# One front instead of three stages: two modulation rows first, the bias between the query and key tiles

## The reference, cut to what matters

```python
ada = jax.nn.silu(c) @ ada_w[l] + ada_b[l]
sh1, sc1, g1, sh2, sc2, g2 = jnp.split(ada, 6, axis=-1)      # six rows of 1024
n1 = rmsnorm(h, norm1_w[l]) * (1.0 + sc1) + sh1
proj = n1 @ w_in[l]                  # 1024 query columns, 1024 key columns, and more
# in the attention, for each query q, key k and head:
bias = bias_table[t5_bucket(positions[k] - positions[q])]    # added to the logits
```

## Time and profile before

| | us |
|---|---|
| median of 3 runs (lowest, highest) | 5376.34 (5373.24, 5382.1) |
| the profiled execution | 5366.34 |
| its span, first to last instruction | 5364.7 |
| PE busy, share of the span | 5029.8, 94% |
| DVE busy, share | 2869.8, 53% |
| ACT busy, share | 1572.6, 29% |

### The profile page before, as it was taken

How to read it: one execution, slowest core, us unless ns; L and a number is a source line. 1 busy time by engine, 2 the same in 40 slices (tenths; PEclk the granted TensorE clock), 3 DMA queues, 4 the chain that set the end, 5 groups by cost and what they waited for, 6 DMA issues and landing times. The chain is left out here.

```text
span 5364.7 us, 69919 instructions
## 1 busy us (share of the span) xinstructions
PE 5029.8 (94%) x25070; PEld 4136.0 (77%) x25070; DVE 2869.8 (53%) x6216; ACT 1572.6 (29%) x2427; POOL 254.4 (5%) x340
## 2 busy tenths in 40 slices
PE   5599979998997998999999999999969999999998
PEld 1388867776886777788888888888858888888887
DVE  6511027776566344466666455555545555555556
ACT  2211125565565332222222222222211111111111
POOL 1100000000333110000000000000000000000000
PEclk8798989999998999999999999999989999999999
DMA  7332123332554552222222243333365555555554
GB/s 292 114 118 89 65 84 122 127 126 102 189 184 144 181 165 75 89 85 91 87 91 95 110 161 140 137 153 144 129 175 142 145 147 142 144 148 142 143 147 132
DMA packets 479906, 710.29 MB, mean 132 GB/s; under 512 B 286432, under 2 KB 334960, under 8 KB 474472
## 3 DMA queue, kind: packets, MB, share of 16 engines
q1 hardware_dynamic: 451080, 598.51, 34.9%
q0 software_dynamic: 22880, 96.79, 5.3%
q10 hardware_dynamic: 5760, 12.59, 0.6%
HBM read 487.32 MB, written 220.49 MB: 132 GB/s over the span
## 5 line engine op out<-in xcount | busy, mean ns | idle before, releaser
L2121 PE MATMUL ph_hid_ps<-ph_n_hi,ph_u_hi 128*128 128x512 f32 x2176 | 855.0, 393 | 8.1 <-ACTq L2196 8.0
L2121 PE MATMUL ph_hid_ps<-ph_n_lo,ph_u_hi 128*128 128x512 f32 x2176 | 847.9, 390 | 0.0
L2121 PE MATMUL ph_hid_ps<-ph_n_hi,ph_u_lo 128*128 128x512 f32 x2176 | 847.8, 390 | 0.0
L2506 PE MATMUL px_out_ps<-px_v_hi,px_weight_hi 128*128 128x512 f32 x2048 | 798.0, 390 | 49.6 <-DVEq L2557 49.6
L2506 PE MATMUL px_out_ps<-px_v_lo,px_weight_hi 128*128 128x512 f32 x2048 | 797.7, 390 | 0.0
L2506 PE MATMUL px_out_ps<-px_v_hi,px_weight_lo 128*128 128x512 f32 x2048 | 797.6, 389 | 0.0
L2585 DVE TENSOR_TENSOR held_tiles<-held_tiles,px_out_ps 128x512 f32<-128x512 f32 x512 | 350.4, 685 | 594.2 <-PE px_out_ps L2506 594.2
L2254 DVE TENSOR_TENSOR ph_u_lo<-ph_u_raw,ph_u_hi 128x1024 fp32r<-128x1024 f32 x136 | 166.7, 1226 | 707.4 <-ACT ph_u_hi L2175 707.0
L2180 ACT ACTIVATE ph_hidden<-ph_hid_ps 128x1024 f32<-128x1024 f32 x128 | 131.2, 1025 | 1209.7 <-PE ph_hid_ps L2121 1209.7
L2506 PEld LDWEIGHTS px_out_ps<-px_v_hi,px_weight_hi 128*128 128x128 f32 x2048 | 385.0, 188 | 129.9 <-DVEq L2557 49.8
L2121 PEld LDWEIGHTS ph_hid_ps<-ph_n_hi,ph_u_hi 128*128 128x128 f32 x2176 | 409.4, 188 | 91.9 <-DVE ph_u_lo L2254 8.3
(11 more groups left out here) (319 smaller groups left out, 7926.2 us busy)
## 6 DMA issues: line engine op xcount, KB each, us to landing
ph_u_raw<-in_tiles SPq DMA_DIRECT2D x136, 512.0 KB, 3.6
scratch_hidden<-ph_hidden SPq DMA_DIRECT2D x128, 512.0 KB, 2.6
scratch_gate_tiles<-ph_gates SPq DMA_DIRECT2D x16, 4096.0 KB, 12.8
px_v_raw<-in_v_experts SPq DMA_DIRECT2D x128, 512.0 KB, 3.5
px_raw<-scratch_hidden SPq DMA_DIRECT2D x128, 512.0 KB, 5.3
px_gate<-scratch_gate_tiles SPq DMA_DIRECT2D x128, 512.0 KB, 6.5
proj_w_ch<-in_w_ch SPq DMA_DIRECT2D x49, 512.0 KB, 3.7
mr_w<-in_ada_w POOLq DMA_DIRECT2D x6, 4096.0 KB, 19.6
```

What stands on the lines that cost most here:

```text
L2121: mm = pe.matmul(hid_ps[r][:, c * HALF:(c + 1) * HALF], u[r][a][:, k, :], n2[b][:, k, c * HALF:(c + 1) * HALF], start=(k == 0 and a + b == ...
L2506: mm = pe.matmul(out_ps[b][:], weight[q][j][wp][:, t * P:(t + 1) * P], v[q][j][vp][:, c * HALF:(c + 1) * HALF], start=(j == 0 and wp + vp ...
```

## The change

Stages one to three become one, `front_and_project` (tiles `fr_`), without barriers between them. Its parts, engine by engine:

- Small constants are laid out on the host into one array `front`, loaded by one DMA; the queries' positions come already repeated.
- `ada_w` is loaded in 12 chunks of 2 MB (three quads of two rows, four chunks each). The four of the first quad go to buffers of their own at once. The other eight go through two buffers, each waiting until the chunk two before it has been multiplied.
- The tokens are multiplied by the norm factor only, turned by PE, and copied to `xT` by ACT (even tiles) and DVE (odd tiles). Afterwards the first quad of rows is computed, turned by four transposes into columns (`cols`), and DVE scales and shifts `xT` block by block (128x512); ACT makes the high and DVE the low part of `n1T`. The adding on POOL is gone.
- Two bias groups come ahead of the turning. The other 62 follow the halves of the 16 query and key tiles, two behind each half. One row chunk follows each of the tiles 1 to 8. The bias results are copied in pieces of up to 512 keys from three PSUM banks.

The core of the diff, the new order on each engine (the long declarations and waits on constants are left out):

```diff
+                def half_tile(n, c):
+                    for k in range(KD):
+                        if n == 0:
+                            pe.wait_ge(n1_lo, c * KD + k + 1)
+                        for a, b in PARTS:
+                            mm = pe.matmul(...)
+                    if c:
+                        mm.then_inc(acc_ready[n % 2], 1)
+                # PE
+                for g in range(AHEAD):
+                    bias_group(g)
+                for t in range(TT):
+                    ...transposes of token tile t
+                for i in range(CHUNKS):
+                    row_chunk(i)
+                pe.wait_ge(first_ready, 1)
+                ...four transposes of the first rows
+                for n in range(TILES):
+                    pe.wait_ge(w_lo[n % 2], n // 2 + 1)
+                    for c in range(2):
+                        half_tile(n, c)
+                        for g in groups_behind(n, c):
+                            bias_group(g)
+                    if 1 <= n <= QUADS * CHUNKS - CHUNKS:
+                        row_chunk(n + 3)
+                # ACT
+                def high(n):
+                    ...
+                        act.wait_ge(w_in[n % 2], n // 2 * 16)
+                        act.wait_ge(acc_ready[n % 2], n // 2)
+                    act.activation(w[n % 2][0][:], w_raw[n % 2][:], ACT.Copy).then_inc(w_hi[n % 2], 1)
+                for n in range(TILES):
+                    for g in groups_behind(n, 0):
+                        take_group(g)
+                    act.wait_ge(acc_ready[n % 2], n // 2 + 1)
+                    act.activation(out[n % 2][:], acc[n % 2][:], ACT.Copy, ...)
+                    if n + 2 < TILES:
+                        high(n + 2)
+                    for g in groups_behind(n, 1):
+                        take_group(g)
+                # DVE
+                def make_steps(g):
+                    if g >= NSTEP:
+                        dve.wait_ge(piece_mm, pieces_until(g - NSTEP + 1))
+                    ...four tensor_scalar of 128 x extent(g), then_inc(steps_ready)
+                def low(n):
+                    dve.wait_ge(w_hi[n % 2], n // 2 + 1)
+                    dve.tensor_tensor(w[n % 2][1][:], ...).then_inc(w_lo[n % 2], 1)
+                full(0)
+                for i in range(2 * KD):
+                    if i + 1 < 2 * KD:
+                        full(i + 1)
+                    dve.wait_ge(n1_hi, i + 1)
+                    dve.tensor_tensor(n1T[1][:, k, cut], xT[:, k, cut], ...).then_inc(n1_lo, 1)
+                for n in range(TILES):
+                    for g in groups_behind(n, 0):
+                        make_steps(g)
+                    if n + 2 < TILES:
+                        low(n + 2)
+                    for g in groups_behind(n, 1):
+                        make_steps(g)
+                # POOL
+                for i in range(6):
+                    load_chunk(i)
+                for n in range(2, TILES):
+                    pool.wait_ge(w_lo[n % 2], n // 2)
+                    pool.dma_start(w_raw[n % 2][:], d["w_ch"][n]).then_inc(w_in[n % 2], 16)
+                    if 6 <= n + 3 < QUADS * CHUNKS:
+                        load_chunk(n + 3)
+        def groups_behind(n, half):
+            at = AHEAD + 4 * n + 2 * half      # AHEAD = 2, NSTEP = 4 buffers of steps
+            return range(at, min(at + 2, GROUPS))
```

More of the change, by code:

```diff
@@ L102, in bucket_starts, with stage_project, front_and_project @@
             for b in range(NB)]
+FRONT_WIDTHS = (P, 1, AH, AH, 1, 3 * KD, KD)
+FRONT_CONSTS = sum(FRONT_WIDTHS)
+FRONT_AT = tuple((sum(FRONT_WIDTHS[:n]), sum(FRONT_WIDTHS[:n + 1])) for n in range(len(FRONT_WIDTHS)))
 def stage_modulation_and_bias(nc, d):
+    pass
+def stage_project(nc, d):
+    with ExitStack() as stack:
+        sp = Space(nc, stack, "proj")
+        with ExitStack() as early:
+            mod_w = early.enter_context(nc.sbuf_tensor("proj_mod_w", [P, 2, 2, 2 * D], F32))
+            xT = early.enter_context(nc.sbuf_tensor("proj_xT", [P, KD, S], F32))
+        n1T = [sp.sb(f"n1T_{part}", [P, KD, S], F32R) for part in ("hi", "lo")]
+        w_ch = [sp.sb(f"w_ch{s}", [P, KD, P]) for s in range(2)]
+        with ExitStack() as tokens:
+            w_tok = [tokens.enter_context(nc.sbuf_tensor(f"proj_w_tok{s}", [P, KD, HALF], F32)) for s in range(2)]
+            w_dt = tokens.enter_context(nc.sbuf_tensor("proj_w_dt", [P, KD, SH], F32))
+            front_and_project(nc, d, n1T, mod_w, xT, w_ch, w_tok, w_dt)
+            project_token_major(nc, d, n1T, w_tok, w_dt, w_ch)
+        attend_and_convolve(nc, d, n1T, w_ch)
+        scan_and_gate(nc, d, n1T, w_ch)
+def front_and_project(nc, d, n1T, mod_w, xT, w_raw, w_tok, w_dt):
     QG = 4
@@ L111, in stage_modulation_and_bias @@
     NJ = QB // QG
-    NBUF = 4
-    N = P // QB // NBUF
-    ROWS = 6
+    NSTEP = 4
+    GROUPS = S // QB
+    AHEAD = 2
     QUADS = 3
-    KC = KD // 2
+    CHUNKS = 4
     TERMS = 3
+    TILES = 2 * AH
+    NBANK = 3
     with ExitStack() as stack:
-        sp = Space(nc, stack, "mr")
-        cT = sp.sb("cT", [P, KD])
+        sp = Space(nc, stack, "fr")
+        consts = sp.sb("consts", [P, FRONT_CONSTS])
+        ident, eps, table, before, first, mod_cols, cT = (consts[:, a:b] for a, b in FRONT_AT)
+        x = sp.sb("x", [P, TT, D])
@@ L138, in stage_modulation_and_bias @@
+        pos_q = sp.sb("pos_q", [P, S // QG], I32)
         pos_k = sp.sb("pos_k", [P, S])
         limit = sp.sb("limit", [P, S // QG])
-        first = sp.sb("first", [P, 1])
-        table = sp.sb("table", [P, AH])
-        before = sp.sb("before", [P, AH])
         diffs_raw = sp.sb("diffs_raw", [P, NB])
         diffs = [sp.sb(f"diffs{n}", [P, NB], BF16) for n in range(TERMS)]
-        steps = [sp.sb(f"steps{s}", [P, NJ, S], BF16) for s in range(NBUF)]
+        w = [[sp.sb(f"w{s}_{part}", [P, KD, P], F32R) for part in ("hi", "lo")] for s in range(2)]
@@ new lines, in front_and_project @@
+        steps = [sp.sb(f"steps{s}", [P, NJ, S], BF16)[:] for s in range(2)] + [
+            x[:, 2 * s:2 * s + 2, :].bitcast(BF16).rearrange("p a (c n) -> p (a c) n", n=S) for s in range(2)]
+        squares = bias_out[1]
+        first_rows = bias_out[1][:, 0:HALF]
+        pos_k_int = out[1][:].bitcast(I32)
+        chunk_to = [w_tok[c][:].rearrange("p k n -> p (k n)").rearrange("p (a n) -> p a n", a=2) for c in range(2)] + [
+            mod_w[:, c, :, :] for c in range(2)]
+        acc = [sp.ps(f"acc{s}", [P, S]) for s in range(2)]
@@ L157, in lane, with pieces, pieces_until @@
+        def pieces(g):
+            return [(c, min(c + HALF, extent(g))) for c in range(0, extent(g), HALF)]
+        def pieces_until(g):
+            return sum(len(pieces(i)) for i in range(g))
+        def groups_behind(n, half):
+            at = AHEAD + 4 * n + 2 * half
+            return range(at, min(at + 2, GROUPS))
         def lane(j):
             return slice(j * NB, j * NB + 1)
[L160 to L166, removed]
@@ L178, in _ @@
[L178 to L188, removed]
@@ new lines, in _ @@
+                for n in range(TILES):
+                    for half in range(2):
+                        if half:
+                            sync.wait_ge(acc_out[n % 2], n // 2 + 1)
+                            sync.dma_start(d["qkT"][n], out[n % 2][:]).then_inc(stored[n % 2], 16)
+                        for g in groups_behind(n, half):
+                            store_group(g)
+                sync.wait_ge(row_step, 6)
+                for j in range(NJ):
+                    sync.dma_start(d["rows"].rearrange("v n -> (v n)").rearrange("(q j n) -> j q n", j=NJ, n=HALF)[j:j + 1, 1:QUADS],
@@ L231, in _ @@
                         st.wait()
[L232 to L243, removed]
@@ L245, in take_rows @@
-                def take_rows(q):
[L246 to L256, removed]
```

520 lines of the change are left out of this document (238 added, 282 removed).

## The result

| | us |
|---|---|
| forecast | 5394, range 5367 to 5420 |
| the new kernel, median of 16 runs | 5383.61 (5379.86 to 5386.16) |
| the kernel before, median of 16 runs | 5376.91 (5367.74 to 5384.3) |
| ratio | 1.0014, interval 1.0007 to 1.0020 |
| span of the profile, after and before | 5380.3 and 5364.7 |

The new kernel is a little slower: 6.7 us by the medians, and 15.6 us by the two profiles; the forecast was 17.4. The interval of the ratio is clear of 1, but 6.7 us is under the 11 us that I had called discernible, so by my own classes the outcome is "same", to which I had given 0.24, and not "slower" with 0.62.

The account below looks back on a forecast made before the run. PE bounds 94% of the span, but not its front. Up to the mark 101+308+20+6.2 = 435.3 against 417.9, +17.4 us: profiled 5366.3 becomes 5384, and 10.0 for the median gives 5394, range 5367 to 5420.

Parts of the forecast that it names:

- the mark: The first token-major matmul, behind which both kernels have the same code: forecast about 435 us against 417.9 before.
- Part 1: Front up to the first tile matmul: loads, early bias pieces, turning, row chunks and a chain, 70 us in all.
- F: Time of the first tile matmul: forecast 70 us, bounds 61 and 78, against 235.0 before.
- Part 2: Tile 0: PE waits for DVE's blocks and the steps behind them; end at F+31 = 101 us, bounds F+27 and F+33.
- Part 3: Tiles to 15: PE waits in each for steps queued behind ACT copy, high part and low part; together 308 us.
- Part 4: PE's clock falls in the waits of nearly each tile: 1.4 us a tile, 20 in all, bounds 0 and 45.
- Part 5: The rest: 6.2 us from tile 15's end to the mark, stores nothing; then the whole sum and the forecast 5394.
- Rival A: Front and tiles: the two gains cancel, about -3 us with the clock alone staying up, 5374; chance 0.20.
- B: Tiles: the bias hides because steps are ready when PE comes to them, 5287; chance 0.10.
- C: Tiles: weights come late behind POOL's row chunk issue, six tiles at 5 us each, +30, 5424; chance 0.12.

Follow-up runs that it names:

- e5: The new kernel with DVE making the steps of tile 0's first two bias groups before it scales the tokens: 5376.52 us.
- e1: The new kernel with the second half's bias steps made before the low part of the weights in DVE's order: 5286.49 us, ratio 0.9841 to the kernel before.
- e3: The new kernel with ACT making the high part of the weights before it copies out the finished tile: 5370.42 us.
- e2: The new kernel with extra PE matmuls, their product overwritten, before the second half's bias groups of tiles 0 to 13: 5366.4 us.
- e9: The new kernel with e1's and e5's orders and POOL issuing each tile's weights ahead of the row chunk: 5281.22 us, ratio 0.9833 to the kernel before.
- e7: The kernel before, unchanged, profiled a third time: span 5376.1 us, DVE beginning at 38.4.
- e11: The kernel before with POOL's third 4 MB row chunk held until the small constants have landed: 5365.55 us, ratio 0.9991 to the kernel before.
- e6: The new kernel with the three order changes of e1, e3 and e5 together: 5284.75 us.

## Why the prediction was right, point by point

The direction is right, the size two and a half times the one measured: 17.4 us against 6.7. On the profiles' own scale, where the sum was made, it is 15.6, and the mark moved by 16.9.

- **Part 1.** F was forecast at 70 and came at 64.2, inside 61 to 78. The tokens landed as forecast (ACT's last square at 36.75), and the fourth bias piece waited 20.32 us on PE for ACT, as told. The square root, 2 us in the sum, took 0.30. But the turning and the row chunks took 12.9 and 7.1 us, not 15.8 and 10: the clock rose during the turning, and from there DVE, which multiplies by the norm factor, set the pace of the turning (PE waits 0.89 to 1.11 for it between tiles). The rows show it by durations (two tiles in 1.97 us, one in 1.94 in the earlier trace rows; a chunk pair in 3.61, the warm value of the earlier trace rows):

```profile
38.77 1.47 PE L323 MATMUL fr_bias_ps<-fr_steps,fr_diffs 128*32 128x512 bf16 x12 [20.32 <-ACT fr_bias_out L392]
...
45.82 1.97 PE L359 MATMUL fr_acc<-fr_consts,fr_x 128*128 128x128 f32 x16 [0.89 <-DVE fr_x L480]
...
52.99 3.61 PE L336 MATMUL fr_row_ps<-proj_w_tok,fr_silu_c 128*1 128x512 f32 x32
```

- **Part 2.** Tile 0 ended 28.1 us behind F, forecast 31 within 27 to 33. DVE made the late steps from 79.6, and the stop was theirs (e5).
- **Part 3.** The step that decides was right. The 14 long waits of PE were 70.5 us; the chains and first groups' steps of the sum are 49.0+24.5 = 73.5. e1 took the wait away and e3 shortened one link by its own length.
- **Part 4.** 20 us were forecast for the clock; e2 bought back 16 to 17. I had read the earlier trace rows too favourably: PE was busy for only 0.49 of the microsecond from 128 and 0.83 of the next before the clock came back, not solidly from 127.0.
- Tiles 1 to 15 took 335.4 us, forecast 328. Without the clock the sum had 308; e2, with the clock up, took 318.0, and e1 and e9 show 11 us more of PE's own work than my terms. So the joints, which I had not priced, cost 10 to 11 us, and the clock 3 less than forecast. Nor do the tile ends fall as told: 24.9 us apart at first and 19.4 at last (before tile 15), not 26 and 17.
- The mark came at 434.8, forecast 435.3. That it agrees within 0.5 is luck: F and tile 0 came 6 and 3 us short, the tiles 7 and the step behind them 1 us long.
- **Part 5, the step that failed.** "The median of the runs shown is 10.0 above the profiled one; on their scale I forecast 5394." I carried the distance between profile and median of the kernel before over to the new one. That distance was no constant: the profile was one of its short executions, and its long ones come in good part from constants held up behind POOL's chunks (e7, e11). The new kernel has its constants in the first three DMAs of SP's queue; DVE has what it needs at 8.5 us, and its times spread by 6 us, not 17. Against e11, the kernel before without the late constants, the new one is 17 to 18 us slower by the medians of different sets, and 13 by the ratios of both to the kernel before; the sum of the prediction was 17.4.

Rival A (the gains cancel) fell with the lowered clock in the windows above. B (the bias hides) was not so here, but e1 has it in another order: forecast 5287, measured 5286.5. That agreement is luck. B's price was 107 us and e1 was worth 97; the 5394 from which it was taken was 10 us too high. C (late weights) did not occur in the new kernel, where POOL's six issues from 128.98 us on come at the end of a stretch of steps or behind it, and took 0.70 to 1.07 us. It appeared in e6, though not in e1 and e9, whose issues do fall amid steps.

The Trainium skill, "SBUF — State Buffer", section "SBUF: two separate sides", says that GpSimd can't write the descriptors of a DMA while DVE runs an instruction in its two-port fast mode. The trace of e6 agrees with its 5.86 us, that of e1 shows issues beside the same steps which were not held up. The Trainium skill, "TensorE: Matmul & The Clock Gate", section "HAM oscillation — how this bites in real kernels", tells of bursts that start cold behind waits of a few microseconds. It bears on part 4, and e2 agrees: the clock stayed up when the waits were filled.

## What to carry to other kernels

Work put "under" a busy engine is hidden only if its inputs are made ahead of the waits of that engine's partner: write down each engine's order, and ask what stands in front of the producer at the moment when the consumer arrives. Here one line of DVE's order was worth 97 us, some 17 of them through the clock that fell in the waits. And look at the spread of the old kernel before adding the distance between its profile and its median to a forecast: a fault that the change removes by the way may be in it.

## What the runs showed of the hardware that was not expected

- The clock rose while PE did nothing but transposes. The first 17 of the new kernel took 0.42 to 0.43 us each on average (40.2 to 43.6 us, lines by form below, first two rows; count | busy, mean ns), the next ones less (third row), and from 45.8 a tile took 0.98 us. In the earlier trace rows transposes stayed at 0.50 for 26 us. There PE was busy 15.7 of 26 us, here solidly from 38.8. The column of the granted clock reads 1.00 from the first instant in both kernels, in the earlier trace rows too, where a row chunk at 15.8 us took 6.27: up to the first change it can't be trusted, and durations must be read.

```profile
L359 PE MATMUL fr_acc<-fr_consts,fr_x 128*128 128x128 f32 x9 | 2.2, 427 | 0.0
L359 PE MATMUL fr_acc<-fr_consts,fr_x 128*128 128x128 f32 x8 | 1.9, 421 | 0.0
L359 PE MATMUL fr_acc<-fr_consts,fr_x 128*128 128x128 f32 x9 | 1.5, 328 | 0.0
```

- SP's queue got 0.3% to 5% of the DMA engines beside 4 MB row chunks of POOL in the kernel before, but a third (0.68 of 2.14 MB in 10 to 15 us) beside the 2 MB chunks of the new one, where its own DMAs are 512 KB. Which of the two sizes does it, no run here separates:

```profile
q0 software_dynamic: 194, 1.46, 68.9%
q1 hardware_dynamic: 189, 0.68, 33.3%
```
